# Where a depthwise convolution of width 31 runs: one channel tile as VectorE taps, the other as TensorE matmuls with diagonal weights

## What is computed

```python
def hybrid_mixer(h, w_in, ...):
    p = h @ w_in
    gq, gk, gv, gr, glr, ca, cg, sq, sk, sv = jnp.split(p, offsets, axis=-1)
    glog = log_sigmoid(glr @ gla_w_gate2 + gla_b_gate) / 16
    o_gla = gla_group(gq, gk, gv, glog, gr, gla_norm_g)   # 4 heads, gated linear attention
    o_conv = conv_group(ca, cg, conv_w, conv_b, conv_ln_g, conv_ln_b)
    o_swa = swa_group(sq, sk, sv, swa_sinks)              # 8 heads, window of 128, a sink logit per head
    return jnp.concatenate([o_gla, o_conv, o_swa], axis=-1) @ w_out

def conv_group(a, g, conv_w, conv_b, ln_g, ln_b):         # 256 channels
    u = a * jax.nn.sigmoid(g)
    y = causal_depthwise_conv(u, conv_w) + conv_b         # width 31
    mu = jnp.mean(y, axis=-1, keepdims=True)
    var = jnp.mean(jnp.square(y - mu), axis=-1, keepdims=True)
    return jax.nn.silu((y - mu) * lax.rsqrt(var + 1e-5) * ln_g + ln_b)
```

## Time and profile before

| | |
|---|---|
| median of 3 runs | 1562.54 us (1562.13 to 1562.94) |
| the profiled execution's own time | 1563.06 us |
| its span | 1560.5 us |
| mean granted TensorE clock | 0.971 |
| TensorE busy | 1474.3 us (94%) |
| VectorE busy | 968.2 us (62%) |
| ScalarE busy | 746.7 us (48%) |
| GpSimd busy | 149.7 us (10%) |

### The profile page before, as it was taken

One profiled execution on the slowest core, in us unless ns is written; L12 is line 12 of the kernel. 1 busy time (PEld: TensorE's weight loads), 2 busy tenths in 40 slices (PEclk: granted clock), 3 DMA queues, 4 the chain that ended last, 5 costly groups with the idle time before them and its releaser, 6 DMA issues. The chain is left out here.

```text
span 1560.5 us, 21647 instructions
## 1 busy us (share of the span) xinstructions
PE 1474.3 (94%) x8994; PEld 1285.8 (82%) x8994; DVE 968.2 (62%) x1174; ACT 746.7 (48%) x966; POOL 149.7 (10%) x104
## 2 busy tenths in 40 slices
PE   6999999899999899998878999999999898899998
PEld 6999999799988788877866888878888687678886
DVE  5766786588854665554765666556654466665644
ACT  4433753455544444345744444454444465454433
POOL 0000000000000000004831000000000275200000
PEclk8999999899999999998989999999999899899999
DMA  7644465566655555455323655547555442265542
GB/s 248 215 131 136 142 204 174 165 176 185 189 189 162 177 187 189 162 164 132 115 66 108 204 188 188 189 137 228 189 176 169 129 129 76 86 207 177 189 154 106
DMA packets 252309, 254.96 MB, mean 163 GB/s; under 512 B 26531, under 2 KB 217396, under 8 KB 252212
## 3 DMA queue, kind: packets, MB, share of 16 engines
q1 hardware_dynamic: 251328, 251.30, 50.9%
q10 hardware_dynamic: 884, 2.28, 0.4%
HBM read 252.50 MB, written 1.05 MB: 162 GB/s over the span
## 5 line engine op out<-in xcount | busy, mean ns | idle before, releaser
L1008 DVE TENSOR_TENSOR w_lo<-raw,w_hi 128x2048 fp32r<-128x2048 f32 (+1 forms) x232 | 533.6, 2302 | 329.8 <-ACT w_hi L617 329.7
L617 ACT ACTIVATE w_hi<-raw 128x2048 fp32r<-128x2048 f32 (+1 forms) x240 | 455.8, 1900 | 354.8 <-PE stream L1673 153.5
L1673 PE MATMUL stream<-a_hi,w_hi 128*128 128x256 f32 (+1 forms) x1056 | 308.0, 292 | 12.0 <-DVE a_lo L1027 8.4
L1673 PE MATMUL stream<-a_lo,w_hi 128*128 128x256 f32 (+1 forms) x1056 | 305.1, 289 | 0.0
L1673 PE MATMUL stream<-a_hi,w_lo 128*128 128x256 f32 (+1 forms) x1056 | 304.9, 289 | 0.0
L1673 PE MATMUL stream<-w_hi,a_hi 128*128 128x512 f32 (+2 forms) x672 | 253.6, 377 | 7.4 <-DVE w_lo L1008 7.4
L1673 PE MATMUL stream<-w_hi,a_lo 128*128 128x512 f32 (+2 forms) x672 | 248.6, 370 | 0.0
L1673 PE MATMUL stream<-w_lo,a_hi 128*128 128x512 f32 (+2 forms) x672 | 248.1, 369 | 0.0
L1673 PEld LDWEIGHTS stream<-a_hi,w_hi 128*128 128x128 f32 (+1 forms) x1056 | 206.3, 195 | 15.9 <-issue 9.2
L1673 PEld LDWEIGHTS stream<-a_lo,w_hi 128*128 128x128 f32 (+1 forms) x1056 | 206.5, 196 | 1.0
L1673 PEld LDWEIGHTS stream<-a_hi,w_lo 128*128 128x128 f32 (+1 forms) x1056 | 206.3, 195 | 1.1
(11 more groups left out here) (285 smaller groups left out, 1753.4 us busy)
## 6 DMA issues: line engine op xcount, KB each, us to landing
raw<-in_ffn_w_up SPq DMA_DIRECT2D x136, 512.0 KB, 5.0
raw<-in_ffn_w_down SPq DMA_DIRECT2D x104, 512.0 KB, 4.4
raw<-in_ffn_w_gate SPq DMA_DIRECT2D x88, 512.0 KB, 4.0
raw<-in_w_in SPq DMA_DIRECT2D x80, 512.0 KB, 4.6
raw<-in_w_out SPq DMA_DIRECT2D x24, 512.0 KB, 4.3
raw<-in_w_ret_o SPq DMA_DIRECT2D x8, 512.0 KB, 4.1
raw<-in_w_lru_o SPq DMA_DIRECT2D x8, 512.0 KB, 4.3
raw<-in_ffn_w_down SPq DMA_DIRECT2D x16, 256.0 KB, 2.8
```

What stands on the lines that cost most here:

```text
L617: nc.scalar.activation(w_hi[s][:, :, 0:n], raw[s][:, :, 0:n], ACT.Copy).then_inc(w_hi_ready, 1)
L1008: V.tensor_tensor(w_lo[s][:, :, 0:n], raw[s][:, :, 0:n], w_hi[s][:, :, 0:n].bitcast(F32), ALU.subtract).then_inc(w_split, 1)
L1673: return nc.tensor.matmul(dst, lhs, rhs, start=start, stop=stop, skip_group_check=True)
```

## The change

- The first feature tile of the convolution is made whole by VectorE: 31 taps in two alternating accumulators, `yc[:, 0]` and `yc_sum`, added at the end. ScalarE's products, GpSimd's ring sums and the ring of buffers are gone.
- The second feature tile is made by TensorE: 31 fp32 matmuls with a 128x128 diagonal matrix of the tap's weights against the shifted input, summed in one half of the PSUM bank `ps7`. They are issued in portions (`conv_taps`) of 3, 2, 6, 6 and 14. ScalarE reads the sum and adds the bias.
- The diagonals are laid out on the host. They are loaded into the tile `diag` (2 MB per layer), which replaces the ring buffers `even` and `odd`, by four DMAs in the first feed-forward of each layer. `diag` shares its memory with `b_hi` and `b_lo`.
- GpSimd's four splits go to VectorE.
- The convolution's statistics steps move from the middle of passes (9,1), (10,0), (11,0) to quarter points: after the first quarter of pass (9,0), after its last, and after the second quarter of pass (9,1).
- Unit 4 is feature-major throughout; the value part is transposed on TensorE and evacuated by ScalarE.
- ScalarE takes over the evacuations of `s_cross`, `vg` and the GLA output `og`; the GLA output moves from `ps7` to `psm` bank 3.
- The sinks of the softmax become a column of the score tile `ss`, so that the maximum and the exponential cover them.
- `hi` and `lo` of some units change their place: on VectorE unit 6 is now split before the first GLA scores, on ScalarE unit 12 now stands behind the tanh of the silu and on VectorE before `b_lo` of the convolution.

```diff
@@ sp, first feed-forward of a layer
+                    if f == 0 and j in (12, 14, 16, 18):
+                        n = 4 * (j - 12)
+                        sp.wait_ge(unit_used, USED[c - UL + UL_WOUT + 3 if l else U1_UP - 1])
+                        sp.dma_start(diag[:, n:n + 8, :], io["conv_diag"][:, l, n:n + 8, :]).then_inc(diag_loaded, 16)
@@ gpsimd
-                split(cm + 3)
-                split(cm + 4)
...
-                split(cm + 6)
-                ring_sums(1, 16)
-                split(cm + 9)
                 power_heads(8)
-                ring_sums(17, RING_SUMS)
@@ scalar
                 hi(cm + 6)
-                products(4)
                 hi(cm + 7)
-                products(8)
+                act.wait_ge(ps7_full, ps70 + PS7_V + 1)
+                nc.scalar.activation(vs[:, :, :], ps7[:, 0:T]..., ACT.Copy).then_inc(ps7_free, 1)
+                act.wait_ge(psm_full, psm0 + PSM_CROSS + 1)
+                nc.scalar.activation(s_cross[:, :, :], psm[:, :, 0:P], ACT.Copy).then_inc(psm_free, 1)
                 hi(cm + 8)
-                products(17)
                 exponentials(0)
+                act.wait_ge(unit_used, USED[cm + 7])
+                act.wait_ge(group_evac, gm + 7)
+                for t in range(TT):
+                    ins = nc.scalar.activation(vg[:, t, :], ..., scale=rs4[:, 2 + t:3 + t])
+                ins.then_inc(group_evac, 1)
                 hi(cm + 9)
-                products(19)
                 exponentials(1)
+                act.wait_ge(gla_full, 2 * l + 1)
+                nc.scalar.activation(sq2[:, :, :], pair2(psm[:, 3, :]), ACT.Square).then_inc(og_sq, 1)
+                nc.scalar.activation(og[:, :, :], pair2(psm[:, 3, :]), ACT.Copy).then_inc(gla_free, 1)
...
+                act.wait_ge(ps7_full, ps70 + PS7_CONV + 1)
+                nc.scalar.activation(yc[:, 1, :], ps7[:, T:2 * T], ACT.Identity, bias=...).then_inc(ps7_free, 1)
...
-                hi(cm + 12)
                 act.wait_ge(silu_in, l + 1)
                 nc.scalar.activation(th2[:, :, :], yc[:, :, :], ACT.Tanh).then_inc(silu_th, 1)
+                hi(cm + 12)
                 operand_hi(b_hi[:, 2:4, :], hn[:, 2:4, :], op(op0 + 2))
@@ vector
+                lo(cm + 3)
...
+                sink_columns()
+                lo(cm + 4)
...
+                lo(cm + 6)
                 gla_scores(0)
...
                 window_scores(0)
                 softmax_shift(0)
                 read_pair(6, qs[:, 2:4, :], SWD ** -0.5)
+                conv(0, 6)
                 window_scores(1)
                 softmax_shift(1)
...
                 softmax_scale(0)
+                lo(cm + 9)
+                conv(6, 14)
...
                 softmax_scale(1)
+                conv(14, 18)
                 (variance of the GLA heads)
                 lo(cm + 10)
                 (gate)
+                conv(18, 24)
                 (og, product)
+                conv(24, 27)
+                lo(cm + 11)
                 operand_lo(b_lo[:, 0:2, :], hn[:, 0:2, :], b_hi[:, 0:2, :])
+                conv(27, TAPS)
+                V.tensor_tensor(yc[:, 0, :], yc[:, 0, :], yc_sum[:, :], ALU.add).then_inc(yc_ready, 1)
...
+                lo(cm + 12)
                 operand_lo(b_lo[:, 2:4, :], hn[:, 2:4, :], b_hi[:, 2:4, :])
@@ tensor
+                def conv_taps(n):
+
+                    pe.wait_ge(up_ready, l + 1)
+                    pe.wait_ge(diag_loaded, 4 * 16 * (l + 1))
+                    pe.wait_ge(ps7_free, ps70 + PS7_CONV)
+                    for tap in range(taken["n"], min(taken["n"] + n, TAPS)):
+                        ins = mm(ps7[:, T:2 * T], diag[:, TAP_SLOT[tap], :], up[:, 1, tap:tap + T], tap == 0, tap == TAPS - 1)
...
                 gla_scores(0)
-                end_pass(token_major((cm + 4) % NS, bank(4), P, P, T, False), cm + 4)
+                second_half(4)
                 unit(5)
                 first_half(5)
                 gla_scores(1)
                 second_half(5)
+                (two transposes of v_t into ps7)
+                conv_taps(3)
                 (cross scores)
                 unit(6)
                 first_half(6)
+                conv_taps(2)
                 window_scores(0)
...
                 (GLA output)
+                conv_taps(6)
                 probabilities(0, [psm[:, m, :] for m in range(3)])
                 (GLA statistics)
+                conv_taps(6)
                 probabilities(1, ...)
                 (broadcast of the root of the GLA heads)
+                conv_taps(TAPS)
                 window_out()
-                conv_steps = {1: conv_mean, 2: conv_variance, 3: conv_root}
+                conv_steps = {(0, 0): conv_mean, (0, 3): conv_variance, (1, 1): conv_root}
```

More of the change, by code:

```diff
@@ L77 @@
 PS7_N0, PS7_SINK, PS7_1 = range(3)
-(PS7_RB, PS7_Z, PS7_PV, PS7_GBC, PS7_L) = range(5)
+(PS7_RB, PS7_Z, PS7_V, PS7_CONV, PS7_L) = range(5)
 ST_RMEAN, ST_RVAR, ST_1 = range(3)
@@ L87 @@
 GATE_UNITS = [U1_END + UL * l + UL_MIX for l in range(LAYERS)]
[L88 to L91, removed]
+TAP_SLOT = (0, 1, 2, 3, 16, 17, 18, 19, *range(4, 16), *range(20, 31))
 def tail_passes(units):
@@ L282, in build, with keys @@
         cg, cub = gu[:, :, 0, :], gu[:, :, 1, :]
+        def keys(slot, n):
+            return ss[:, slot, n * (P + 1):n * (P + 1) + P]
         def mx_half(row, b):
@@ L1743, in deep_pass @@
                         ins = mm(y_bank(t, n), lo_t[:, k, tok], h[:, j, cols], False, last and j == 1)
-                    if last and n == 0:
-                        ins.then_inc(half_done, 1)
-                    if n == 0 and between:
-                        between()
-                end_pass(ins, c, t)
+                        if n + j == 2:
+                            end_pass(ins, c, t)
+                        elif last and (n, j) == (0, 1):
+                            ins.then_inc(half_done, 1)
+                        if between[2 * n + j]:
+                            between[2 * n + j]()
             def turn(i, t, src):
@@ L2043, in _ @@
                 second_half(5)
+                pe.wait_ge(group_evac, gm + 5)
+                pe.wait_ge(ps7_free, ps70 + PS7_V)
+                for t in range(TT):
+                    ins = nc.tensor.transpose(cols(ps7, t), cols(v_t, t), ident)
+                ins.then_inc(ps7_full, 1)
+                conv_taps(3)
                 psm_ready(PSM_CROSS)
@@ L2062, in _ @@
                     for t in range(TT):
-                        mm(ps7[part, at + t * P:at + t * P + P], vg[0:64, t, v], s_gla[0:64, t, h, :], h < 2 and t == 0, False)
-                    ins = mm(ps7[part, at + P:at + T], vg[:, 0, v], s_cross[:, h, :], False, False)
+                        mm(gla_out[part, at + t * P:at + t * P + P], vg[0:64, t, v], s_gla[0:64, t, h, :], h < 2 and t == 0, False)
+                    ins = mm(gla_out[part, at + P:at + T], vg[:, 0, v], s_cross[:, h, :], False, False)
                 ins.then_inc(near_done, 1)
@@ L2071, in _ @@
                         late = slice(at + t * P + 64, at + t * P + P)
-                        ins = mm(ps7[part, late], vg[64:P, t, v], s_gla[64:P, t, h, 0:64], False, h > 1 and t == 1)
-                ins.then_inc(ps7_full, 1)
-                psm_ready(PSM_L)
+                        ins = mm(gla_out[part, late], vg[64:P, t, v], s_gla[64:P, t, h, 0:64], False, h > 1 and t == 1)
+                ins.then_inc(gla_full, 1)
+                conv_taps(6)
                 probabilities(0, [psm[:, m, :] for m in range(3)])
@@ L2096, in _ @@
                         at = 4 * t + 2 * f
-                        ins = mm(ps7[:, at:at + 2], cols(sq2[:, f, :], t), headsel, at == 0, at == 6)
+                        ins = mm(gla_out[:, at:at + 2], cols(sq2[:, f, :], t), headsel, at == 0, at == 6)
                 ins.then_inc(stat_full, 1)
-                probabilities(1, [psm[:, 3, :], stream[2][:, :], stream[0][:, :]])
+                conv_taps(6)
+                pe.wait_ge(group_evac, gm + 9)
+                probabilities(1, [stream[m][:, :] for m in (2, 0, 1)])
                 pe.wait_ge(rstd8_ready, l + 2)
@@ L2139, in _ @@
                     deep_pass(c, t, b_hi, b_lo, range(2 * m, 2 * m + 2), c == cm + 9, c == cm + 12, branch_ready,
[L2140 removed]
+                              {n: conv_steps.get((step, n)) for n in range(4)})
                 ffn(c0 + UL_UP_B, 2 * l + 1, i + 2, (lambda: turn(i + 2, 0, x_t)) if l < LAYERS - 1 else None)
```

179 lines of the change are left out of this document (69 added, 110 removed).

## The result

The changed kernel takes 1538.7 us (median; 1537.2 to 1539.8) against 1562.7 (1562.1 to 1563.8) on the same chip: ratio 0.9845, 95% interval 0.9828 to 0.9862, so 24.1 us faster. The forecast was 1540, range 1531 to 1552. The profiled execution took 1539.7 us, its span 1537.6.

The account below looks back on a forecast made before the run. TensorE was taken as the bound: -50.3 us of waits and slow clock, +23.8 of TensorE work and +4.0 of new waits gave -22.5. The forecast was 1540 us, range 1531 to 1552.

Parts of the forecast that it names:

- The waits and the clock: TensorE's standstills in the mixer and half clock behind them: at most 26.5 us to win in layer 0, 23.8 in layer 1.
- new waits: TensorE waits that the change itself brings into the mixers: 2.0 us a layer, 4.0 together.
- the round trip of `v`: Taps in the mixer wait for ScalarE's copy of the transposed `v`: 0.5 us, between 0 and 1.
- the GLA scores: Second GLA scores wait for the evacuation of the first, behind VectorE's split of unit 6: about 0.5 us.
- the last branch: End of the mixer: the 3.1 us wait for `b_lo` shrinks to 0 to 1.4, taken as 1 us.
- TensorE's work: Each mixer: 31 taps add 14.0 us, unit 4 gives back 2.4, transposes of `v` cost 0.3: 11.9 more.
- The margins of VectorE: At the first branch: `b_lo` 2.9 us early, the convolution 1.4, so the waits of 5.2 and 2.5 go.
- rival B: The branches' waits stay because VectorE is over 8 us late in each layer: 4.7 us slower, 1567; chance 0.07.
- Rival A: The last branch stays late, GpSimd's root drawn out beside VectorE's split: 8.7 us more, 1549; chance 0.22.
- Moved without a price: Splits moved to VectorE and eight diagonal loads in the feed-forward cost nothing; loads costing 20 us given 2 in 100.
- Rival C: No waits at all in the mixers, taps at 0.39 us: 1532; chance 0.13.
- D: Half of the gain is lost to waits not seen in advance: 1552 to 1563; chance 0.06.

Follow-up runs that it names:

- e2_unit12_early: The changed kernel with only `hi` and `lo` of unit 12 back in their old places: 1545.8 us, ratio 0.9890.
- e1_steps_late: The changed kernel with the convolution's three statistics steps and unit 12's `hi` and `lo` back in their old places: 1545.7 us, ratio 0.9894.
- i4_mended: The changed kernel reordered against small waits, with the transposes of `v` ahead of every tap: 1536.0 us, ratio 0.9823.
- i6_12_taps_on_vector: i4_mended with 12 of the second tile's 31 taps moved to VectorE and unit 11's split behind the centring: 1525.8 us, ratio 0.9758.
- e6_no_ring: The kernel before the change without ScalarE's products and GpSimd's running sums (24 taps left out), GpSimd's splits kept: 1540.2 us, ratio 0.9848.
- e3_9_taps: The changed kernel with taps 8 to 29 of the second tile left out, 9 remaining on TensorE: 1535.1 us, ratio 0.9824.
- e5_gpsimd_splits: e4_vg_on_vector with the splits of units 3, 4, 6 and 9 back on GpSimd: 1543.3 us, ratio 0.9870.
- e4_vg_on_vector: The changed kernel with `vg` evacuated by VectorE again, before the scaling of the first softmax: 1538.2 us, ratio 0.9839.
- e7_small_sums: The kernel before the change, products and splits kept, each of GpSimd's 22 running sums cut from 512 to 2 columns: 1546.5 us, ratio 0.9890.
- i1_small_waits: The changed kernel with three taps before the transposes of `v` and unit 6 split after the first GLA scores: 1536.6 us, ratio 0.9824.

## Why the prediction was right

**The waits and the clock.** Forecast: 26.5 us in layer 0 and 23.8 in layer 1 to be won, with 2.0 us of new waits each. Of the four waits over 2 us (5.2, 3.6, 3.1 and 2.5) 0.3 is left, and the clock is 1.00. The mixer of layer 0 was forecast at 87 us and took 85.7. The new waits are 1.3 us: the round trip of `v` 0.6 (forecast 0.5), the GLA scores 0.4 (0.5), the last branch 0.3 (1.0).

**TensorE's work.** Forecast +11.9 us a layer. The taps took 14.03 (forecast 14.0). Unit 4's second half and unit 5's first take 748.30 - 741.89 - 0.39 of waiting = 6.02 us, against 5.41 + 3.02 before: 2.4 us back, as forecast. Checked as a whole: busy time in layer 0 was 82.4 us, with 9.7 us of loss by slow clock in it if half clock doubles the time (the forecast's estimate; the last section has what was measured); now it is 84.5, which is 84.5 - 72.7 = 11.8 more. The value 0.45 was right, but its reason only for a small part: I took it, and not 0.39, because of the changes between kinds of work. The portion of 14 takes 0.446 a tap too, the small ones 0.49 and 0.48, so a tap costs about 0.44 and a portion some 0.1 on top, 0.5 of the 14.0 us. The 0.39 came from a group of two matmuls, too short to read a rate from the earlier trace rows.

**The margins of VectorE.** The forecast had `b_lo` of the first branch 2.9 us early and the convolution 1.4. Measured from the timeline of VectorE:

```profile
799.82 0.68 DVE L975 TENSOR_TENSOR b_lo<-hn,b_hi 128x512 fp32r<-128x512 f32 x1
...
801.61 0.48 DVE L1452 SCALAR_TENSOR_TENSOR yc<-up,vecs,yc 128x256 f32<-128x256 f32 x1
802.12 0.43 DVE L1583 TENSOR_TENSOR yc<-yc,yc_sum 128x256 f32<-128x256 f32 x1
```

The branch starts at 804.07 and its convolution mean at 804.89, so they are 3.6 and 2.3 us early. VectorE's taps follow each other at 0.40 us, where 0.45 was taken. It was these margins that decided against rival B, and the kernels with 8 and 12 more taps on VectorE found their end.

**The last branch** was the step right in its sum and thin in its reason. I let unit 12's two operations be a burden on the convolution's chain (2.3 to 4.2 us onto 5.2) and credited the quarter points with the room. The chain was 7.7 us long (810.11 to 817.83, start of the broadcast to start of the branch) over a cover of 7.4, and so just fitted. But e2_unit12_early shows that the quarter points alone do not do it: with unit 12 at its old place 7.1 us are lost. What I priced as a burden, the later place of the split, is what the step cannot do without. That the early statistics are needed beside it was not tested alone.

Rival A had about the right size (1549; e1 and e2 gave 1545.7 and 1545.8). Its mechanism, the root drawn out by VectorE's split, is there in e1_steps_late (2.68 us, with 0.2 us of TensorE waiting for it), and so its reason against itself, that the split is moved behind the root, was the right one: in the changed kernel the root takes 0.70 us. What it did not see is the way of e2_unit12_early: the root is as short there, and VectorE is held up in its own queue by a split whose `w_hi` is not yet to be had.

**The place of the gain.** I put the gain down wait by wait. The runs give its shares in the two mixers together:

| kernel | mixers, us | less than before |
|---|---|---|
| before | 196.1 | |
| sums of GpSimd cut short | 178.1 | 18.0 |
| sums and products removed | 176.0 | 20.1 |
| the change | 171.4 | 24.7 |
| i4_mended | 169.0 | 27.1 |
| i6_12_taps_on_vector | 160.4 | 35.7 |

Nearly three quarters of what the change wins (18.0 of 24.7; by the medians 17.0 of 24.1) would be won by taking the long additions off GpSimd, 23 in each layer, whatever became of the taps. The change then pays 24 us of TensorE work net for the second tile's taps, and gets that back and 4.6 us more from what e6_no_ring still has: 9.0 us of waits in layer 0 and a mean clock of 0.94 and 0.92. By the medians it is only 1.5 us more, and the intervals of the two overlap. e3_9_taps shows that this payment is in good part cover: in layer 0 9.8 us of work less saved 3.0 us.

**Moved without a price.** The eight loads of diagonals cost nothing that can be seen: the stretch between the mixers, with four of them, is 0.4 us shorter. Giving GpSimd its four splits back costs 6.8 us in the mixers and 5.1 by the medians (e5_gpsimd_splits against e4_vg_on_vector), so that this part of the change was itself a gain; I had only priced it as harmless, beside the wait for `vg`.

**Rival C** (no waits, taps at 0.39) did not come in: most of the waits did vanish, but the taps took 0.45. **D** saw waits that return; there were 1.3 us of them in a layer. **B** put VectorE over 8 us late; it was 3.6 us early at the first branch.

## What to carry to other kernels

Look first at who shares something with the engine that is late: a helper engine at 10% busy can cost much (here 18 us in the two mixers), so measure it by cutting its instructions short while keeping their number and waits. When work is moved onto the engine that bounds a stretch, put it where that engine would have waited, and then move it off again piece by piece until the first small wait returns. And an early result is only early if no instruction that waits for something later is queued ahead of its use.

## What the runs showed of the hardware

**GpSimd and VectorE.** Beside a long GpSimd operation a short VectorE operation can last until that one ends: 0.17 us became 4.47 in the earlier trace rows and 2.80 in e5_gpsimd_splits, where both ends lie within 0.02 us. Not every operation is held up: the two reductions beside the split in e5_gpsimd_splits took 1.22 and 0.68 us, as in the changed kernel. The expectation of that run named operations with two SBUF inputs; the subtraction of the earlier trace rows reads two tiles, the change of sign that was held up in e5_gpsimd_splits (2.80 us) only one. What decides which operation is held up was not shown. Long VectorE operations suffer as well: its splits took a mean of 2.83 us in the mixer of layer 0 before, 2.28 in e7_small_sums and 2.29 in the changed kernel, and its taps 0.67 us before and 0.48 in both others. It goes the other way too: GpSimd's root of two columns took 2.68 us beside VectorE's split (e1_steps_late) and 0.70 without one (e2_unit12_early).

**The same pause, another clock.** A wait of 1.6 us in e5_gpsimd_splits was followed by 10.6 us at a mean clock of 0.52 in layer 0 and by no slow clock in layer 1 (1.00 through the mixer). A wait of 3.1 us before the last branch was followed by slow clock in the kernel before (5.9 us at 0.50) and by full clock in layer 0 of e6_no_ring (8.3 us at 1.00, 816.1 to 824.4). The prediction had pauses up to 2.5 us as harmless; the length of the pause alone does not decide it. What does was not found.

**What half clock costs.** The losses given here and in the prediction take it that at half clock the work takes twice the time. That is an estimate. fp32r matmuls of 256 columns followed each other at 0.214 us at a clock of 0.50 (before, 783.22 to 787.92, 1.2 columns per ns) and the same ones at 0.119 us at 1.00 (changed kernel, 778.64 to 781.26); those of 512 columns at 0.427 us and 0.227 us (before, 827.19 to 831.46 and 834.01 to 835.60). That is 1.79 and 1.88 times, so 44 to 47% of the slow time was lost and not 50: 8.5 to 9.1 us instead of 9.7 in layer 0 of the kernel before.

**Two sums in one PSUM bank.** In i1_small_waits three taps were accumulated into the right half of a bank, then two transposes were written into the left half, and the accumulation went on in the right. The run's output is what the reference gives with taps 0 to 2 of the second tile set to zero in both layers: relative to the full reference both differ by 0.139871. So behind the transposes in one half of the bank the next matmul in the other half overwrote the open sum instead of adding to it: exactly the three taps before them are gone. i4_mended, with the transposes ahead of all taps, has the same length of the mixers (84.5 us) and no such loss.
